# Halving the head's input projection, four modulation units on VectorE, and decay sums ahead of level products

## The reference

```python
def trunk_layer(x, cond, p, ...):
    mod = (silu(cond) @ p['w_ada'] + p['b_ada'])[:, None, :]          # 6 * 1024 columns for each of the two groups
    sh1, sc1, g1, sh2, sc2, g2 = jnp.split(mod, 6, axis=-1)
    h = rmsnorm(x, p['norm1']) * (1 + sc1) + sh1
    q, k, v, gq, gk, gv, gg, lr_f, lr_b, ga, gb = _split_proj(h @ p['w_in'])
    o_attn = block_attention(norm_rope(q), [norm_rope(k), ctx_k], [v, ctx_v])
    la_f = log_sigmoid(lr_f @ w2[0] + b[0]) / 16                      # la_b likewise
    o_gla, s_f, s_b = bidirectional_gla(gq, gk, gv, la_f, la_b, s0_f, s0_b)
    o_gla = rmsnorm(o_gla, p['gla_norm']) * silu(gg)
    merged = sigmoid(ga) * (o_attn @ p['w_pa']) + sigmoid(gb) * (o_gla @ p['w_pb'])
    x = x + g1 * (merged @ p['w_out'])
    h2 = rmsnorm(x, p['norm2']) * (1 + sc2) + sh2
    return x + g2 * grouped_moe(h2, router_w, router_bias, p['w_gate'], p['w_up'], p['w_down'])
```

## Time and profile before

| | |
|---|---|
| Median of 3 runs | 1046.28 us (1043.95 to 1046.61) |
| The profiled execution | 1045.26 us, of it 1043.5 us span from the first to the last instruction |
| TensorE busy (matmuls) | 973.5 us, 93% |
| VectorE, ScalarE, GpSimd busy | 346.9, 239.3, 101.9 us |
| Moved by DMA | 316.44 MB, mean 303 GB/s |
| Chain that ended last | TensorE 72%, DMA 14%, VectorE 7%, ScalarE 4% |

### The profile page before, as it was taken

The page is one execution under the profiler, slowest core; times in us unless marked ns, Lnnn a source line. Parts: engine busy times, 40 slices in busy tenths (PEclk is TensorE's granted clock), DMA queues, the critical chain, the costliest instruction groups (busy, mean ns, idle before and its releaser), DMA issues.

```text
span 1043.5 us, 13728 instructions
## 1 busy us (share of the span) xinstructions
PE 973.5 (93%) x4974; PEld 569.9 (55%) x4974; DVE 346.9 (33%) x944; ACT 239.3 (23%) x524; POOL 101.9 (10%) x82
## 2 busy tenths in 40 slices
PE   5899999998998999999999999999899899999987
PEld 2348877664864543443354588766587454344333
DVE  2116113682352222221161431237734402222224
ACT  1213222522012221221141122233201132121111
POOL 0000003751100000000000000056311000000000
PEclk9999999999999999999999999999999999999999
DMA  9974332249999999899998434240757999989992
GB/s 392 426 294 188 131 120 111 94 164 431 399 363 401 412 421 422 365 421 421 423 426 373 179 149 145 98 161 1 311 206 291 407 405 423 422 360 421 422 422 108
DMA packets 36835, 316.44 MB, mean 303 GB/s; under 512 B 4192, under 2 KB 4336, under 8 KB 5168
## 3 DMA queue, kind: packets, MB, share of 16 engines
q1 hardware_dynamic: 35856, 311.28, 72.9%
q0 software_dynamic: 928, 4.47, 1.0%
HBM read 313.88 MB, written 1.85 MB: 303 GB/s over the span
## 4 chain that ended last, share of the span: by engine, by line
PE 72%; DMA 14%; DVE 7%; ACT 4%; issue 2%; SPq 1%; ACTq 0%; DVEq 0%
PE ps L917 18%; DMA ring<-w_gu 11%; PE ps L506 11%; PE ps L613 8%; PE ps L929 7%; PE ps L806 5%; PE ps L875 3%; PE ps L792 3%; DMA ring<-w_in 3%; PE ps L631 3%; PE ps L724 2%; PE ps L486 2%; PE ps L890 1%; PE ps L519 1%; PE ps L662 1%
## 5 line engine op out<-in xcount | busy, mean ns | idle before, releaser
L917 PE MATMUL ps<-ring,tmq 128*64 128x512 f32 x928 | 215.7, 606 | 16.6 <-DMA ring<-w_gu 13.1
L917 PEld LDWEIGHTS ps<-ring,tmq 128*64 128x64 f32 x928 | 68.6, 139 | 144.2 <-issue 125.5
L506 PE MATMUL ps<-more,ring 128*128 128x256 f32 x512 | 114.3, 381 | 0.5 <-ACT more L986 0.5
L929 PE MATMUL ps<-ring,tmq 128*64 128x512 f32 x512 | 113.8, 596 | 0.0
L506 PEld LDWEIGHTS ps<-more,ring 128*128 128x128 f32 x512 | 96.1, 190 | 15.5 <-issue 2.6
L613 PE MATMUL ps<-ring,more 128*128 128x512 f32 (+1 forms) x256 | 99.1, 548 | 1.6 <-DMA ring<-w_in 1.6
L986 ACT ACTIVATE tmq<-ps 128x256 f32<-128x256 f32 (+3 forms) x124 | 55.6, 462 | 162.9 <-PE ps L613 88.0
L1709 DVE TENSOR_TENSOR tmq<-tmq,ps 128x256 f32<-128x256 f32 x32 | 13.5, 421 | 207.8 <-ACT tmq L1237 207.8
L613 PEld LDWEIGHTS ps<-ring,more 128*128 128x128 f32 x256 | 48.8, 192 | 50.6 <-issue 47.0
L929 PEld LDWEIGHTS ps<-ring,tmq 128*64 128x64 f32 x512 | 35.2, 137 | 65.7 <-issue 62.0
L1720 DVE SCALAR_TENSOR_TENSOR x<-ps,mod,x 128x128 f32<-128x128 f32 x256 | 67.6, 342 | 1.9 <-PE ps L875 1.9
(11 more groups left out here) (235 smaller groups left out, 980.5 us busy)
## 6 DMA issues: line engine op xcount, KB each, us to landing
ring<-w_gu SPq DMA_DIRECT2D x116, 1024.0 KB, 14.2
ring<-w_down SPq DMA_DIRECT2D x64, 1024.0 KB, 12.6
ring<-w_ada SPq DMA_DIRECT2D x24, 2048.0 KB, 11.9
ring<-w_in SPq DMA_DIRECT2D x16, 2048.0 KB, 18.5
ring<-w_out SPq DMA_DIRECT2D x4, 2048.0 KB, 12.5
more<-w_gu SPq DMA_DIRECT2D x8, 1024.0 KB, 14.4
cst<-consts SPq DMA_DIRECT2D x2, 2080.0 KB, 27.3
ring<-w_pa SPq DMA_DIRECT2D x2, 2048.0 KB, 8.3
```

Source lines behind the costliest of these rows:

```text
L506: mm = pe.matmul(ps[:, 5, i * NT:(i + 1) * NT], w[:, k, m * P:(m + 1) * P], h[:, k, :], start=k == 0, stop=k == KT - 1)
L917: mm = pe.matmul(ps[r:r + SLOTS, half, :].rearrange("p (j n) -> p j n", j=2), hg[:, k, e, 0:SLOTS], gu_unit(l, kh, e, in_more)[:, part, :, ...
L929: mm = pe.matmul(ps[r:r + SLOTS, 2 + n, :], at_[:, k, r:r + SLOTS], down_unit(l, k // 2)[:, e, k % 2, n * 512:(n + 1) * 512], start=k == 0 ...
```

## The change

**Head, layer 0.** The four ada units come in the order 0, 2, 1, 3, and between the second and the third of them the first halves (input channels 0 to 511) of the units `in` 0 and `in` 1 are loaded; their second halves follow behind unit 3. TensorE does the first halves of chunks 0 to 3 from tiles 0 to 3 between the ada units, then the second halves. The gains are formed in two halves. VectorE adds the squares of all tiles together, so that one matmul against ones is left. The late constants are loaded ahead of `gates` 0, and lparams after the halves, its state part only after ada 7.

**Ada 4 to 7 of layer 0 on VectorE.** Their weights lie transposed in memory: partition = output column. The two conditioning vectors are turned by TensorE, copied by ScalarE, written to HBM and read back to all partitions (`cs_rows`, 1024 KB), by GpSimd's queue, after the halves. Each unit then takes 4 blocks of 2 instructions, product and sum over 1024 elements (32 instructions in all), and a bias. They stand in VectorE's order as 4 blocks after the modulation, 4 while it waits for the root of the QK norm, 2 before the k copies, 5 behind them and 1 after the first block's softmax. The ring order puts them behind the head's six units, behind `in` 3, and behind `gates` 0 and 1; a unit's slot is free when VectorE is through with it. The fill list of layer 0 keeps only ada 8 to 11, in the places of 4 to 7, and nothing is left after the last GLA pair. TensorE's ada 8 waits for ada 7 (they share `wide`).

**Both layers.** `gla_in(i + 1)` stands ahead of `gla_levels(i)`.

The core of the diff:

```diff
+FIRST_ADA = (0, 2, 1, 3)
+HALVED = [(0, "in", 0), (0, "in", 1)]
+VECTOR_ADA = (4, 5, 6, 7)
...
     if l + 1 < LAYERS:
-        return gates + [ada[4], HOLE, pa[0], HOLE, pa[1], HOLE, ada[5], HOLE, pa[2], HOLE, pa[3], HOLE, ada[6], HOLE,
-                        ada[7], ada[8], ada[9], ada[10], ada[11]]
+        return gates + [ada[8], HOLE, pa[0], HOLE, pa[1], HOLE, ada[9], HOLE, pa[2], HOLE, pa[3], HOLE, ada[10], HOLE,
+                        ada[11]]
...
-    out = [(0, "ada", a) for a in range(4)]
+    out = [(0, "ada", a) for a in FIRST_ADA[:2]] + HALVED + [(0, "ada", a) for a in FIRST_ADA[2:]]
     for l in range(LAYERS):
         out += [(l, "ada", a) for a in early_units(l)]
-        out += [(l, "in", n) for n in range(len(IN_UNITS))]
+        if l == 0:
+            out.append((l, "ada", VECTOR_ADA[0]))
+        for n in range(len(IN_UNITS)):
+            if (l, "in", n) not in HALVED:
+                out.append((l, "in", n))
+            if l == 0 and n == 3:
+                out.append((l, "ada", VECTOR_ADA[1]))
...
             elif kind == "gate" and n % 2 == 0:
                 out.append((l, "gates", n // 2))
+                if l == 0 and n in (0, 2):
+                    out.append((l, "ada", VECTOR_ADA[2 + n // 2]))
...
+                    load(ORDER[n], slice(0, UNIT // 2) if ORDER[n] in HALVED else slice(None), dense_full[n % RING])
                     n += 1
                     if n == RING:
-                        sp.dma_start(cst[:, C_LATE:CW], consts[:, C_LATE:CW]).then_inc(in_d, 16)
+                        for key in HALVED:
+                            load(key, slice(UNIT // 2, UNIT), in_late)
...
+                if l == 0:
+                    ada_a(l, FIRST_ADA[0])
+                    pe.wait_ge(sq_dve, 1)
+                    pe.matmul(ps[:, 0, 0:NT], ones, h[:, 0, :], start=True, stop=True).then_inc(ssum, 1)
+                    pe.matmul(ps[0:KT * S, 5, 0:P], sm[:, 0:KT * S], ident, start=True, stop=True).then_inc(g_nt, 1)
...
+                if l == 0:
+                    ada_b(l, FIRST_ADA[0])
+                    ada_a(l, FIRST_ADA[1])
+                    ada_b(l, FIRST_ADA[1])
+                    first_half(0)
+                    first_half(1)
+                    ada_a(l, FIRST_ADA[2])
+                    first_half(2)
+                    ada_b(l, FIRST_ADA[2])
+                    ada_a(l, FIRST_ADA[3])
+                    ada_b(l, FIRST_ADA[3])
+                    first_half(3)
+                    for n in range(4):
+                        second_half(n)
...
                     fill(l)
-                    gla_levels(i)
                     if i < 7:
                         gla_in(i + 1)
+                    gla_levels(i)
...
+            def ada_blocks(l, count):
+                for _ in range(count if l == 0 else 0):
+                    a, i = blocks.pop(0)
+                    n = PLACE[(l, "ada", a)]
+                    w = ring[:, n % RING, :].rearrange("p (i k) -> p i k", i=4)
+                    if i == 0:
+                        dve.wait_ge(in_lp, loaded(l, "cs_rows"))
+                        dve.wait_ge(dense_full[n % RING], 16 * (n // RING + 1))
+                    for s in range(S):
+                        link(dve.scalar_tensor_tensor(wide[:, :], w[:, i, :], 1.0, cs_rows[:, s, :], ALU.mult, ALU.mult,
+                                                      accum_out=mod[:, l, 4 * a + i, s:s + 1]))
...
+                ada_blocks(l, 4)
+                dve.wait_ge(in_c, 16)
                 dve.wait_ge(proj_copied, TM_CHUNKS * l + 4)
...
-                inv_rms(QK_RMS, HD, sm[:, 32:52], RSQ * l + 2)
+                inv_rms(QK_RMS, HD, sm[:, 32:52], RSQ * l + 2, lambda: ada_blocks(l, 4))
...
                 ins.then_inc(gg_ready, 1)
+                ada_blocks(l, 2)
                 dve.wait_ge(gqk_mm, 2 * l + 2)
...
                 ins.then_inc(gk_copied, 1)
+                ada_blocks(l, 5)
```

More of the change, by code:

```diff
@@ L102, with ada_turn, on_vector, tensor_turn @@
 HOLE = ("none", 0)
+FIRST_ADA = (0, 2, 1, 3)
+HALVED = [(0, "in", 0), (0, "in", 1)]
+VECTOR_ADA = (4, 5, 6, 7)
+CS_ROWS = 1
+def ada_turn(l, a):
+    return l * ADA + (FIRST_ADA.index(a) if l == 0 and a < len(FIRST_ADA) else a)
+def on_vector(l, a):
+    return l == 0 and a in VECTOR_ADA
+def tensor_turn(l, a):
+    turn = ada_turn(l, a)
+    return turn - sum(ada_turn(0, i) < turn for i in VECTOR_ADA)
+POOL_LOADS = [["cs_out", "cs_rows", "lparams", "state", "shift_out", "shift_rows"],
+              ["lparams", "shift_out", "shift_rows"]]
+def loaded(l, name):
+    return 16 * (sum(len(names) for names in POOL_LOADS[:l]) + POOL_LOADS[l].index(name) + 1)
 def fill_list(l):
@@ L1299, in one_over_one_plus, with squares, gains @@
                 link(dve.reciprocal(ap, ap))
-            def squares():
-                dve.tensor_tensor(h[:, 6:KT, :], x[:, 6:KT, :], x[:, 6:KT, :], ALU.mult).then_inc(sq_dve, 1)
-            def gains(l, n):
-                dve.wait_ge(ada_mod, l * ADA + (4 if n == 0 else 10))
-                norm = PR("norm1" if n == 0 else "norm2")[:, l * KT:(l + 1) * KT]
-                c = mod[:, l, 24 * n + 8:24 * n + 16, :]
-                link(dve.tensor_scalar(modA[:, n, :, :], c, 1.0, None, ALU.add))
-                dve.tensor_tensor(modA[:, n, :, :], modA[:, n, :, :], each(norm, [P, KT, S]),
-                                  ALU.mult).then_inc(gain_ready, 1)
-                dve.wait_ge(gain_ready, 2 * l + n + 1)
+            def squares(l):
+                ins = dve.tensor_tensor(h[:, 6:KT, :], x[:, 6:KT, :], x[:, 6:KT, :], ALU.mult)
+                if l == 0:
+                    link(ins)
+                    dve.wait_ge(sq_act, 3)
+                    for n in (4, 2):
+                        link(dve.tensor_tensor(h[:, 0:n, :], h[:, 0:n, :], h[:, n:2 * n, :], ALU.add))
+                    ins = dve.tensor_tensor(h[:, 0, :], h[:, 0, :], h[:, 1, :], ALU.add)
+                ins.then_inc(sq_dve, 1)
+            def gains(l, n, ks=slice(0, KT), turn=None):
+                norm = PR("norm1" if n == 0 else "norm2")[:, l * KT:(l + 1) * KT][:, ks]
+                c = mod[:, l, 24 * n + 8:24 * n + 16, :][:, ks, :]
+                to = modA[:, n, ks, :]
+                link(dve.tensor_scalar(to, c, 1.0, None, ALU.add))
+                dve.tensor_tensor(to, to, each(norm, [P, ks.stop - ks.start, S]), ALU.mult).then_inc(gain_ready, 1)
+                dve.wait_ge(gain_ready, turn or gain_turn(l, n))
             def norm_sum(l):
                 if l:
+                    dve.wait_ge(ada_mod, l * ADA + 4)
                     gains(l, 0)
@@ L1318, in norm_sum @@
                 inv_rms(BIG_RMS, D, ps[:, 0, 0:NT], RSQ * l + 1)
-                scaled(4)
-                scaled(0)
-                if not l:
-                    scaled(6)
-                    scaled(2)
+                for k in (4, 0) if l else (0, 2):
+                    scaled(k)
             def scaled(k):
@@ L1329, in norm_mod @@
             def norm_mod(l):
-                if not l:
-                    gains(l, 0)
                 done = 4 * l
@@ L1766, in _ @@
             for l in range(LAYERS):
+                late = 0 if l else GH * DV
                 if l:
                     pool.wait_ge(x_done, l)
-                pool.dma_start(lpar, lparams[l]).then_inc(in_lp, 16)
+                else:
+                    pool.wait_ge(g_nt_copied, CS_ROWS)
+                    pool.dma_start(cs_dram.rearrange("s k p -> k s p"), shift_row).then_inc(in_lp, 16)
+                    pool.wait_ge(in_lp, loaded(l, "cs_out"))
+                    pool.wait_ge(in_late, HALVES_IN)
+                    pool.dma_start(cs_rows, cs_dram.rearrange("s k p -> s (k p)").unsqueeze(0).to_broadcast([P, S, D])
+                                   ).then_inc(in_lp, 16)
+                    pool.wait_ge(in_lp, loaded(l, "cs_rows"))
+                pool.dma_start(lpar[:, late:LW], lparams[l, :, late:LW]).then_inc(in_lp, 16)
                 pool.wait_ge(k_normed, 2 * l + 1)
```

155 lines of the change are left out of this document (102 added, 53 removed).

## The result

| | before | after |
|---|---|---|
| median of 4 runs each, same chip | 1046.11 us (1043.95 to 1046.61) | 1027.24 us (1026.01 to 1027.79) |
| ratio after / before, 95% | | 0.9825 [0.9813, 0.9837] |
| profiled execution: time, span | 1045.26, 1043.5 | 1027.79, 1025.6 |
| mean granted clock of TensorE | 0.989 | 0.989 |

What follows compares the result with a forecast made beforehand. TensorE's chain was taken to bound the mixers, alternating with w_gu loads in the experts. Terms 1.3 - 3.8 - 1.7 + 10.1 - 0.7 + 2 x 2.4 gave 10.0 us less, median 1036.3, range 1027 to 1046.

Steps and rivals of the forecast that it cites:

- The stop behind the head: Ahead of layer 0's decay projection, TensorE waits 3.8 us for VectorE's ada products, then loses 1.7 at the lower clock.
- The price of a product: VectorE's product with sum over 1024 elements, in ada 4 to 7, takes 1.26 us, bounds 1.2 and 2.33.
- The rival that cost 18 us: VectorE's product with sum takes 2.33 us, so the kernel gets 8.4 us slower, 1054.7; chance 0.10.
- The tail: End of layer 0's GLA stage: four ada units leave TensorE, last gla_out to w_pb 6.3 for 16.4, 10.1 us won.
- slow start of w_pb: After the stop at the end of layer 0's mixer, w_pb may start slowly: 0.7 us lost, half of 1.4.
- the loads would swallow it: Rival: expert loads don't start earlier, so the 10.1 us is given back and 1046 comes out; chance 0.06.
- The head: Start of layer 0: input projection chunks end at 61.6 against 62.84, 1.3 us less.
- The order: GLA stages: decay sums ahead of level products fill TensorE's waits, 2.4 us won per layer, at most 3.6.
- VectorE in time: Rival: ada 5 lands in time or TensorE keeps its clock in the head, 1027 to 1031 us; chance 0.17.

Runs made afterwards that it cites:

- e3: Changed kernel with ada unit 5 loaded one place earlier, ahead of the short unit in 3: 1024.51 us, ratio 0.9795.
- e4: Changed kernel with all four head ada units loaded and worked ahead of the half units: 1021.39 us, ratio 0.9774.
- e6: Changed kernel with 13 unread matmuls of 416 columns in TensorE's idle places in the head: 1023.12 us, ratio 0.9787.
- e7: Changed kernel with unread matmuls in the head's idle places and ada 5 loaded ahead of in 3: 1023.56 us, ratio 0.9805.
- e5: Changed kernel with 15 unread matmuls behind layer 0's last GLA head, where the four ada units stood: 1037.45 us, ratio 0.9931.
- e1: Kernel before with one edit, the next head's decay sums ahead of the level products in both layers: 1034.58 us, ratio 0.9896.
- e2: Changed kernel with level products ahead of the next head's decay sums again: 1039.87 us, ratio 0.9936.

## Why the prediction was right, and where it was not

**The stop behind the head: right, with its cause.** Forecast 3.8 and 1.7 for the lower clock; measured 3.89, then 2.90 + 14.79 for 1.98 + 13.98 at the upper level, 1.7. The chain that was forecast (H, the end of chunk 3, + 8.3 for the load + eight products + the QK norm) is on VectorE's timeline line by line, and e3 shows which link binds: the landing. With an earlier head another one does (e4, e6, e7): cs_rows, which landed at 49.8 where 47.5 was forecast, and VectorE's work behind it.

**The price of a product: right.** 1.27 from one to the next (forecast 1.26). The rival that cost 18 us is refuted for this form: the profile has no such instruction over 1.23. By the rule of the Trainium skill cited in the prediction (Vector Engine (DVE) Microarchitecture Reference, "Points that are easy to get wrong") it would have been 2.33, and this trace does not agree with it. The accumulator's reading is indeed a separate instruction, as that rival had it, but it costs 0.01 in the chain: products start 1.27 apart with it and 1.26 without.

**The tail: right.** 10.3 by the difference of 16.4 and 6.06 (forecast 10.1). The 0.7 for a slow start of w_pb did not come in layer 0. Its whole price is 1.75 and not 1.4: the prediction took two rows of 7.17 for the 64 matmuls, which in a row take 13.98 (at 86.97, before), against 15.74. That the loads would swallow it is refuted by e5, which gave 10.8 back and lost 9.8 at the experts of layer 0 and 9.7 at those of layer 1.

**The head: right in kind, 0.7 off.** 60.80 for H = 61.6, a gain of 2.0 for 1.3. What holds it back was named (half clock, copy, turn and bias in a row), and e6 and e4 put sizes on it: 5.0 us of it goes when TensorE stays busy, 2.6 when the ada units simply come first.

**The order: the step that failed.** The term was 2.4 per layer, the measurement 4.7, above even the bound of 3.6. Two things went wrong in it. First, I took 1.2 off for waits that come or stay (0.2 in three heads, 0.6 in the last). After shows 0.6 ahead of L841, of which 0.2 stood there before, and 0.2 ahead of L818, so 0.6; and 0.6 that the kernel before had elsewhere, ahead of L734 (0.8 to 0.2), is gone, which I had not seen would go. Idle time fell by 3.7, most of the 4.85 there was. Second, 1.0 us of what counts as busy time went, which the sum had no term for, and so the bound was no bound: I reckoned with waits alone, "nothing is removed". The timeline of head 1 has part of it, first of the kernel before, with the earlier trace rows between the two lines, then of after:

```profile
182.91 0.66 PE L495 MATMUL ps<-cst,adarow 128*128 128x128 f32 x4
...
187.82 3.62 PE L519 MATMUL ps<-more,ring 128*128 128x256 f32 x16
```

```profile
186.40 0.66 PE L551 MATMUL ps<-cst,wide 128*128 128x128 f32 x4
186.99 0.88 PE L797 MATMUL ps<-cst,mixer 64*64 64x384 f32 x8
187.79 0.66 PE L803 MATMUL ps<-cst,mixer 128*64 128x128 f32 x8
188.38 1.83 PE L818 MATMUL ps<-mixer 128*128 128x128 f32 x14
...
190.38 3.62 PE L575 MATMUL ps<-more,ring 128*128 128x256 f32 x16
```

From the turn to the fill behind the level products it was 4.91 with a wait of 0.75 in it, so 4.16, and is 3.98 with the same matmuls in the other order: 0.18 in one head. No matmul got shorter: the mean durations of the large groups are the same in both kernels (0.508 and 0.285 for the sums, 0.280 and 0.282 for the level products), so what fell is the time in which only one of them is under way. TensorE's records leave 11 gaps in the stage before and 6 after, and at a gap the last matmul overlaps with nothing. That this makes the 1.0 is a reading, not shown: the trace models the ends of matmuls, and no run took it apart. Nor was it tested whether VectorE's and GpSimd's shorter instructions (2.7 and 1.9 us less, in e1 as well) are a cause of the gain or come with it. That the order brings all 4.7 is shown, by e1 and e2, from both sides.

**Luck of the clock.** Between the start of layer 0's experts and layer 1's input projection the difference grows from 11.5 to 12.7. The kernel before has a lower-level stretch at 515 there that after lacks, both behind the same wait of 2.56 for a w_gu load, first before, then after:

```profile
513.86 8.78 PE L917 MATMUL ps<-ring,tmq 128*64 128x512 f32 x32 [2.56 <-DMA ring<-w_gu]
...
502.83 7.09 PE L1011 MATMUL ps<-ring,tmq 128*64 128x512 f32 x32 [2.56 <-DMA ring<-w_gu]
```

I know of nothing in the change that bears on it.

**The sum.** Against the forecast of 10.0: order 2 x 2.3 more, head 0.7, the slow start 0.7, tail 0.2, the clock 1.7; that is 7.9 more and makes the 17.9 of the spans (0.5 given back in layer 0's experts and 0.5 won at the end of the span cancel). The medians are 1.0 further apart. The range held, barely, because it reached down for a rival that did not come true (VectorE in time), and that is luck; with 4.7 for 3.6 as the order's bound its low end would have been near 1025.

## What to carry to other kernels

Where an engine waits a microsecond at a time for a product made next door, look for work of the next round that needs nothing of it and put it in front: here two swapped lines are worth half of a large change, and the sum of such waits is not the upper bound of the gain. When work is moved to an idle engine, follow its load and the ring slot that the load waits for, not only the engine's time: the stop that the moved units caused was a landing, and one place in the load order took it away. Then look again: once the head was faster, that landing bound nothing, and the wait was for the engine's work behind another one. And price a stretch of TensorE behind idling at the lower clock; before threading work into such a stretch, try it behind.

## What the runs showed of the hardware

Matmuls whose product nobody reads, put where TensorE idles in the head, made it faster: the granted clock stood at its upper level from the first unit on (1.92 for 3.64, 7.10 for 8.80), and the chunks ended 5.0 us earlier (e6). A lower-level stretch cost 1.7 us where the same matmuls stand at both levels: 8.80 for 7.1 behind a stop of 1.62 (head), 8.78 for 7.09 behind 2.56 (experts, before). Not every such stop is followed by one: behind the 2.56 in the experts there is none after, and behind the 1.82 at the end of the GLA stage there is one in layer 1 (15.73 for 13.98) and none in layer 0 (7.17).

On VectorE, a product with its sum over 1024 float32 elements, both sources in SBUF, took 1.23 us, a plain product 1.22.
